# Moving columns and PSUM columns taken in other orders of 64-byte lines

## The chip, the cores and the metric

The kernel runs on one core of one Trainium2 chip. The metric is the device time of one execution in microseconds; of several executions the median is given. Nothing but the order in which TensorE takes the columns of its 256-column products differs between the two kernels.

## The reference, cut to what matters

256 tokens of width 1024 pass through two blocks, all in float32:

```python
# first block, 256 tokens and 256 of context
x  = x + 0.5 * gate * swiglu(modulate(rms_norm(x)), ffn1_w_in, ffn1_w_out)     # the context too
bg, cg, vc, q, k, v, gt = split(modulate(rms_norm(x)) @ w_in)
x  = x + gate * merge(conv_branch(bg, cg, vc), attention(q, k, v), gt)
x  = x + 0.5 * gate * swiglu(modulate(rms_norm(x)), ffn2_w_in, ffn2_w_out)
x  = rms_norm(x)
# second block
x  = x + rms_norm(concat(mlstm(...), stick_breaking(...)) @ w_out_ab)          # even layer, from x @ w_in_ab
x  = x + rms_norm((pool_mix(p) * silu(z)) @ w_out_c)                           # odd layer, from x @ w_in_c
```

Nearly all arithmetic is in the products of activations with weight matrices, each of which is used once.

## The kernel before, in words

Each float32 product is made of three products of type fp32r (float32 rounded so that TensorE takes it in one pass): weights and activations are each split into a high and a low part, and high*high, high*low and low*high are summed in PSUM. For weights, ScalarE writes the high part WH (line 1565) and VectorE the low part WL (line 1988), one "chunk" of 4 x 128 x 256 weights at a time, from a ring W of eight buffers that the SP queue fills from HBM. Activations lie turned, features on the partitions and tokens along the free axis, as pairs of buffers: XH and XL inside XHB and XLB, GH and GL (hidden layer of the two feed-forward parts), YH/YL, OH/OL, ZH/ZL, RH/RL, PH/PL.

`Plan` writes the order of all work as a list of steps. A step "ck" is one chunk of one `Gemm`. A Gemm has a kind ("fa1", "q", "cg", ...), an index i of its 256 weight columns, and `cols`, the token columns it is made for: (0, 512) in the first feed-forward part and for k and v (latent and context tokens together), 256 columns everywhere else. `chunk(s)` in the TensorE program issues it: for each 128 weight columns j and each 128 rows k three matmuls, lines 1105, 1106, 1107. The stationary operand is 128 x 128 of WH or WL (eight 64-byte lines of every partition), loaded by an LDWEIGHTS that comes with each matmul; the moving operand is one row of the activation buffer, 256 or 512 tokens of four bytes (16 or 32 lines); the output is as many columns of one PSUM bank, of four that are used in turn. A Gemm whose `turned` is false (v, ev, sv, p1) has the two roles the other way round, lines 1111 to 1113. Small products of plain float32 (attention, sums of squares, the mLSTM) stand between, on other lines.

A Gemm with eight 128-row blocks has 2 x 8 x 3 = 48 matmuls. The stages, in order of time: first feed-forward part (fa1, fb1, fx1; its last group of columns, made by `halves`, in two passes of 256 tokens) to 392 us; q, then k and v to 446; cg, vc, bg to 532; gt and mc to 593; ga to 622; ma to 644; res to 667; second feed-forward part (fa2, fb2, fx2) to 855; even layer (eq, ek, ev, eo, ez, then sq, sk, sv, sz) to 1101; p0 to 1150; odd layer (op, oz, om) to 1272; p1 to 1315.

Where the buffers start, in units of a 64-byte line (16 columns): XHB and XLB hold the first moving buffer at columns 0 and 80 and the later one, XH and XL, at columns 48 and 0. The buffers of the other stages follow a pad each in one common place: 16 columns of pad ahead of GH[1] and GL[1], 64 columns ahead of YH, of GH[2], of ZH and of RH. So GH[1] and GL[1] begin on a line of the other parity than GH[2], YH, OH, ZH, PH, XH and XL do; WH and WL stay where they are, and by the kernel's sizes lie at the same parity as GH[1] and at the other parity than the rest.

Of the kernel before, what the change touches and what calls it, by code (L numbers as in the profile page):

```python
# [15 lines left out]
T = 256  # L16
# [856 lines left out]
def build_program(nc, w, out):  # L873
    with ExitStack() as ctx:
# [95 lines left out]
        def parts(j):  # L970
# [5 lines left out]

        MOVING = {"fa1": (X1H, X1L), "fb1": (X1H, X1L), "fx1": (GH[1], GL[1]), "fx2": (GH[2], GL[2]), "mc": (YH, YL), "ma": (OH, OL), "res": (YH, YL),
                  "p0": (ZH, ZL), "p1": (RH, RL)}
        SHADE = {4: T, 5: T}
        NORMED = {1: 0, 2: 16, 3: 32, 4: 40, 5: 48}  # L980
        READY = {"fa1": ("nl", 0), "q": ("nl", 16), "fa2": ("nl", 32), "eq": ("xr", 0), "ev": ("nl", 40), "oz": ("nl", 48), "mc": ("yl", 0),
# [22 lines left out]
        def _(sp):  # L1004
# [39 lines left out]
                             X[:, 4 * j + 2 * a:4 * j + 2 * a + 2, 0:T]).then_inc(S["out"], 16)  # L1044
            sp.wait_ge(S["out"], 16 * 4)

        @block.tensor
        def _(pe):
            def ones(name, i):
# [18 lines left out]
            def chunk(s):  # L1068
                gm = s.gemm
                kind, (a, b) = gm.kind, gm.cols  # L1070
                if kind == "om":
                    xh, xl = PH[:, gm.g % 2, :, :], PL[:, gm.g % 2, :, :]
                else:
                    xh, xl = MOVING.get(kind, (XH, XL))
                _, h, l = parts(s.chunk)
                pe.wait_ge(S["wl"], s.chunk + 1)
                order = [(j, k) for j in range(len(gm.tiles)) for k in range(s.nk)]
                if gm.first:
                    order.sort(key=lambda o: o[1])
                if s.b:  # L1080
                    order = [o for o in order if o[1] == s.b - 1]
                if s.half >= 0:
                    order = order[len(order) // 2 * s.half:len(order) // 2 * (s.half + 1)]
                for j, k in order:
                    t, kk = gm.tiles[j], s.k0 + k
                    ps = P[:, t % 4, :]
                    if kk == 0 and t >= 4:
                        name, v = plan.tile_free[t - 4]
                        pe.wait_ge(S[name], v)
                    if gm.first and j == 0 and not (kind == "oz" and gm.raw):  # L1090
                        if kind in ("fa1", "fb1"):
                            pe.wait_ge(S["nl"], 2 * kk + 2)
                        elif kind == "k":
                            pe.wait_ge(S["nl"], NORMED[2] + 8 + kk + 1)
                        elif kind in ("fx1", "fx2"):
                            pe.wait_ge(S["hl" + kind[2]], gm.g + kk + 1)
                        elif kind == "om":
                            pe.wait_ge(S["pl"], 4 * gm.g + kk + 1)
                        else:
                            name, v = ("xr", 8) if kind == "op" and gm.raw else READY[kind]  # L1100
                            pe.wait_ge(S[name], v + kk + 1)
                    if gm.turned:
                        o = ps[:, 0:b - a]
                        c = slice(j * 128, j * 128 + 128)
                        pe.matmul(o, h[:, k, c], xh[:, kk, a:b], start=kk == 0, stop=False)  # L1105
                        pe.matmul(o, h[:, k, c], xl[:, kk, a:b], start=False, stop=False)  # L1106
                        mm = pe.matmul(o, l[:, k, c], xh[:, kk, a:b], start=False, stop=kk == gm.nk - 1)  # L1107
                    else:
                        o = ps[:, 0:256]
                        c = slice(a + j * 128, a + j * 128 + 128)  # L1110
                        pe.matmul(o, xh[:, kk, c], h[:, k, :], start=kk == 0, stop=False)  # L1111
                        pe.matmul(o, xh[:, kk, c], l[:, k, :], start=False, stop=False)  # L1112
                        mm = pe.matmul(o, xl[:, kk, c], h[:, k, :], start=False, stop=kk == gm.nk - 1)  # L1113
                    if kk == gm.nk - 1 or (k == s.nk - 1 and j == len(gm.tiles) - 1):
                        mm.then_inc(S["g"], 1)
                    if kk == gm.nk - 1 and kind in SUMS and (kind[:2] != "fx" or gm.g == 12):
                        m = gm.i + j if kind[:2] == "fx" else 2 * gm.i + j
                        if m == 6 or m == 7 and kind != "fx2":
                            ones(SUMS[kind], m - 6)
# [13 lines left out]
            for s in seq:  # L1133
# [5 lines left out]
                elif s.kind == "s1":  # L1139
                    pe.wait_ge(SI[1], 16)  # L1140
                    pe.wait_ge(S["sf"], 3 * s.a + 3)
                    for t in range(2):
                        for i in range(2):
                            c = T * i + 128 * t
                            mm = pe.matmul(P[:, s.a, t:t + 1], SQ1[:, s.a, 0, c:c + 128], con("one", 0, 1),
                                           start=i == 0, stop=i == 1)
# [6 lines left out]
                elif s.kind == "mm":  # L1153
                    pe.wait_ge(S["sc"], 1)
                    for r in range(2):
# [7 lines left out]
                        for k in range(4):  # L1163
                            mm = pe.matmul(ps[32 * k:32 * k + 32, 0:256], SCP[:, 4 * r + k, :], src[:, k, :],
                                           start=r == 0, stop=r == 1)
                        mm.then_inc(S["mm"], 1)
                elif s.kind == "mt":
                    pe.wait_ge(S["mr"], 2 * s.a + 2)
                    for g in range(2):
                        for j in range(2):  # L1170
                            n = 2 * g + j
                            mm = pe.transpose(ps[:, 128 * n:128 * n + 128],
                                              ROW[:, (2 * s.a + 1 - g) % 4, 128 * j:128 * j + 128], con("id"))
# [93 lines left out]
                elif s.kind == "m0":  # L1267
                    h = s.a
# [1116 lines left out]
```

## Time and profile before

| | us |
|---|---|
| median of 3 runs | 1329.38 |
| lowest, highest | 1324.02, 1330.24 |
| the profiled execution | 1324.45 |
| its span, first to last instruction | 1322.6 |
| TensorE busy | 1304.7 (99%) |
| weight loads busy | 1210.0 (91%) |
| VectorE busy, ScalarE busy | 903.0 (68%), 644.3 (49%) |

TensorE's matmuls are pipelined: each is shown longer than the distance at which they start. For 256 columns the profile shows 276 to 283 ns of duration, while the starts lie 113 to 120 ns apart. The distance from start to start, called the pitch below, is what a matmul costs in a stream.

### The profile page before, as it was taken

What the parts mean: (1) busy time and instruction counts of PE and PEld (TensorE: products, weight loads), DVE (VectorE), ACT (ScalarE), POOL (GpSimd) and SP (SyncE); (2) the same over time, 40 slices, a digit from 0 to 9 for tenths busy, and PEclk for the clock granted to TensorE, in tenths of its full rate; (3) what the DMA queues carried; (4) which work ended last, traced back from release to release, by engine and by line L of the source; (5) the groups of instructions that cost most, each with busy time, mean ns of one, the idle gap of its engine ahead of it and who ended that gap; (6) DMA issues with size and microseconds to landing.
All of it is one profiled execution on the core that took longest, in us unless ns stands there. A gap on an engine that the chain in (4) does not pass through costs nothing. (4 is left out here: it accounts for less than half of the span.)

```text
span 1322.6 us, 23508 instructions
## 1 busy us (share of the span) xinstructions
PE 1304.7 (99%) x9348; PEld 1210.0 (91%) x9348; DVE 903.0 (68%) x1455; ACT 644.3 (49%) x1027; POOL 27.3 (2%) x27
## 2 busy tenths in 40 slices
PE   9999999999999999999999999999999999999998
PEld 6788888888889999999999999989999999999998
DVE  4768775555658587554775555788887665689873
ACT  4622311222236345554555445666665765556552
POOL 0000000000010000000000000200000000100000
PEclk9999999999999999999999999999999999999999
DMA  9755555646635354545556665556546455436760
GB/s 358 270 186 191 191 191 192 222 159 215 204 107 161 111 159 130 159 128 160 178 155 194 190 201 174 171 159 184 148 143 181 128 174 176 145 112 208 217 197 33
DMA packets 201485, 230.20 MB, mean 174 GB/s; under 512 B 7073, under 2 KB 191649, under 8 KB 201377
## 3 DMA queue, kind: packets, MB, share of 16 engines
q1 hardware_dynamic: 201088, 228.42, 54.7%
q8 instruction: 75, 1.23, 0.4%
q10 hardware_dynamic: 288, 0.28, 0.1%
q14 instruction: 34, 0.27, 0.1%
HBM read 227.63 MB, written 1.05 MB: 173 GB/s over the span
## 5 line engine op out<-in xcount | busy, mean ns | idle before, releaser
L1105 PE MATMUL P<-XHB,WH 128*128 128x256 f32 (+1 forms) x1808 | 553.1, 306 | 7.4 <-DVE XLB L1784 3.9
L1106 PE MATMUL P<-XLB,WH 128*128 128x256 f32 (+1 forms) x1808 | 543.2, 300 | 0.0
L1107 PE MATMUL P<-XHB,WL 128*128 128x256 f32 (+1 forms) x1808 | 543.2, 300 | 0.0
L1988 DVE TENSOR_TENSOR WL<-W,WH 128x1024 fp32r<-128x1024 f32 x358 | 431.7, 1224 | 87.2 <-ACT WH L1565 87.0
L1565 ACT ACTIVATE WH<-W 128x1024 fp32r<-128x1024 f32 x358 | 369.0, 1042 | 249.3 <-PE P L1107 157.8
L1105 PEld LDWEIGHTS P<-XHB,WH 128*128 128x128 f32 x1808 | 340.0, 188 | 27.7 <-issue 8.2
L1106 PEld LDWEIGHTS P<-XLB,WH 128*128 128x128 f32 x1808 | 340.1, 188 | 15.2 <-issue 0.5
L1107 PEld LDWEIGHTS P<-XHB,WL 128*128 128x128 f32 x1808 | 340.2, 188 | 14.6
L1105 PE MATMUL P<-GH,WH 128*128 128x256 f32 (+1 forms) x372 | 121.2, 326 | 0.0
L1106 PE MATMUL P<-GL,WH 128*128 128x256 f32 (+1 forms) x372 | 120.6, 324 | 0.0
L1107 PE MATMUL P<-GH,WL 128*128 128x256 f32 (+1 forms) x372 | 120.6, 324 | 0.0
L1858 DVE TENSOR_TENSOR TS<-TS,P 128x512 f32<-128x512 f32 (+1 forms) x44 | 24.4, 554 | 84.1 <-PE P L1107 84.1
L1106 PEld LDWEIGHTS P<-GL,WH 128*128 128x128 f32 x372 | 70.0, 188 | 6.4 <-issue 0.2
L1105 PEld LDWEIGHTS P<-GH,WH 128*128 128x128 f32 x372 | 70.0, 188 | 6.3 <-DVE WL L1988 0.2
L1107 PEld LDWEIGHTS P<-GH,WL 128*128 128x128 f32 x372 | 70.0, 188 | 6.1
L2058 DVE CUSTOM_DVE_ANT_0 W<-W,AC,V 128x1024 f32<-128x1024 f32 x56 | 71.5, 1277 | 0.0
L1424 ACT ACTIVATE GH<-TS 128x512 fp32r<-128x512 f32 (+1 forms) x44 | 23.0, 524 | 90.1 <-DVE TS L1858 90.1
L1418 ACT ACTIVATE TS<-P 128x512 f32<-128x512 f32 (+1 forms) x44 | 21.5, 491 | 84.6 <-PE P L1107 84.5
L1868 DVE SCALAR_TENSOR_TENSOR X<-P,GM,X 128x256 f32<-128x256 f32 x48 | 21.2, 479 | 52.1 <-PE P L1107 52.0
L1111 PE MATMUL P<-WH,XHB 128*128 128x256 f32 x160 | 45.7, 285 | 1.4 <-DVE WL L1988 1.1
L1112 PE MATMUL P<-WL,XHB 128*128 128x256 f32 x160 | 44.6, 279 | 0.0
L1113 PE MATMUL P<-WH,XLB 128*128 128x256 f32 x160 | 44.6, 279 | 0.0
(322 smaller groups left out, 1797.3 us busy)
## 6 DMA issues: line engine op xcount, KB each, us to landing
W<-in_ffn_w_in SPq DMA_DIRECT2D x88, 512.0 KB, 4.8
W<-in_w_in_ab SPq DMA_DIRECT2D x72, 512.0 KB, 4.6
W<-in_w_modt SPq DMA_DIRECT2D x56, 512.0 KB, 3.9
W<-in_w_in SPq DMA_DIRECT2D x52, 512.0 KB, 4.1
W<-in_ffn_w_out SPq DMA_DIRECT2D x40, 512.0 KB, 4.8
W<-in_w_in_c SPq DMA_DIRECT2D x32, 512.0 KB, 4.3
W<-in_w_out_ab SPq DMA_DIRECT2D x16, 512.0 KB, 4.4
W<-in_w_out_c SPq DMA_DIRECT2D x16, 512.0 KB, 4.7
```

Of the source, the lines that this page charges most:

```text
L1105: pe.matmul(o, h[:, k, c], xh[:, kk, a:b], start=kk == 0, stop=False)
L1106: pe.matmul(o, h[:, k, c], xl[:, kk, a:b], start=False, stop=False)
L1107: mm = pe.matmul(o, l[:, k, c], xh[:, kk, a:b], start=False, stop=kk == gm.nk - 1)
L1111: pe.matmul(o, xh[:, kk, c], h[:, k, :], start=kk == 0, stop=False)
L1112: pe.matmul(o, xh[:, kk, c], l[:, k, :], start=False, stop=False)
L1113: mm = pe.matmul(o, xl[:, kk, c], h[:, k, :], start=False, stop=kk == gm.nk - 1)
L1418: act.activation(TS[:, f % NS, 0:n], ps, ACT.Silu).then_inc(S["sil" + kind[2]], 1)
L1424: act.activation(GH[m][:, f % 12, :], TS[:, f % NS, 0:n], ACT.Copy).then_inc(S[f"hh{m}"], 1)
L1565: act.activation(h, a, ACT.Copy).then_inc(S["wh"], 1)
L1858: dve.tensor_tensor(TS[:, f % NS, 0:n], TS[:, f % NS, 0:n], ps, ALU.mult).then_inc(S[f"hm{m}"], 1)
L1988: dve.tensor_tensor(l, a, h.bitcast(F32), ALU.subtract).then_inc(S["wl"], 1)
L2058: td = dve.tensor_tensor_reduce(a if v == s.c - 1 else JK[:, :, :], a, (AC0, AC1)[v][:, :, :], 1.0, vec("bmod", 8 * g + k), ALU.mult, ALU. ...
```

## The change

Every product in lines 1105 to 1107 that has 256 moving columns takes these columns in another order, by kind. The same order is used for the moving operand and for the PSUM output, so each column lands where it did. Products of 512 columns and those that are not turned stay. No instruction, wait or transfer is added or taken away.

```diff
+        WAYS = {"q": "even", "cg": "back", "vc": "back", "bg": "back", "gt": "pairs", "mc": "even", "ga": "quads", "ma": "pairs",
+                "res": "back", "eq": "even", "ek": "even", "ez": "back", "sq": "pairs", "sk": "pairs", "sz": "even",
+                "p0": "back", "op": "even", "oz": "pairs"}
...
+        def way(gm):
+            if gm.kind in ("fa2", "fb2"):
+                return ("plain", "even", "back", "pairs", "quads", "twos", "eights")[gm.i // 2 % 7]
+            if gm.kind == "fx2":
+                return ("even", "back", "pairs", "quads")[gm.i // 2]
+            return WAYS.get(gm.kind, "plain")
+        def in_order(a, kind):
+            if kind == "even":
+                return a.rearrange("p (l e c) -> p e l c", e=2, c=16)
+            if kind == "pairs":
+                return a.rearrange("p (l e c) -> p e l c", e=2, c=32)
+            if kind == "twos":
+                return a.rearrange("p (l e c) -> p e l c", e=2, c=2)
+            if kind == "eights":
+                return a.rearrange("p (l e c) -> p e l c", e=2, c=8)
+            if kind == "quads":
+                return a.rearrange("p (l e c) -> p e l c", e=4, c=16)
+            if kind == "back":
+                return a[:, ::-1]
+            return a
...
                         o = ps[:, 0:b - a]
+                        mh, ml = xh[:, kk, a:b], xl[:, kk, a:b]
+                        if b - a == T:
+                            o, mh, ml = (in_order(v, way(gm)) for v in (o, mh, ml))
                         c = slice(j * 128, j * 128 + 128)
-                        pe.matmul(o, h[:, k, c], xh[:, kk, a:b], start=kk == 0, stop=False)
-                        pe.matmul(o, h[:, k, c], xl[:, kk, a:b], start=False, stop=False)
-                        mm = pe.matmul(o, l[:, k, c], xh[:, kk, a:b], start=False, stop=kk == gm.nk - 1)
+                        pe.matmul(o, h[:, k, c], mh, start=kk == 0, stop=False)
+                        pe.matmul(o, h[:, k, c], ml, start=False, stop=False)
+                        mm = pe.matmul(o, l[:, k, c], mh, start=False, stop=kk == gm.nk - 1)
```

With the 16 lines of a row numbered from 0: "even" takes lines 0, 2, ... 14, then 1, 3, ... 15; "pairs" 0, 1, 4, 5, 8, 9, 12, 13, then 2, 3, 6, 7, ...; "quads" 0, 4, 8, 12, then 1, 5, 9, 13, and so on; "eights" the first half of every line, then the second halves; "twos" columns 0, 1, 4, 5, 8, 9, ..., then 2, 3, 6, 7, ...; "back" columns 255 down to 0.

## Rows read from the trace of the kernel before

**Rows 1.** The page: span, busy shares, TensorE's row and granted clock in 40 slices.
```profile
span 1322.6 us, 23508 instructions
...
PE 1304.7 (99%) x9348; PEld 1210.0 (91%) x9348; DVE 903.0 (68%) x1455; ACT 644.3 (49%) x1027; POOL 27.3 (2%) x27
...
PEclk9999999999999999999999999999999999999999
```

**Rows 2.** Waits of TensorE, the longest: total us, times, longest us.
```profile
PE P L1105 <- DVE XLB L1784: 3.9, 3, 1.5
```

**Rows 3.** TensorE in order of time, near 700 us (start us, us): second feed-forward part.
```profile
700.09 0.28 PE L1105 MATMUL P<-XHB,WH 128*128 128x256 f32 x1
...
701.45 0.28 PE L1105 MATMUL P<-XHB,WH 128*128 128x256 f32 x1
```

**Rows 4.** The same near 626 us: the products "ma".
```profile
625.75 0.28 PE L1105 MATMUL P<-OH,WH 128*128 128x256 f32 x1
...
627.52 0.28 PE L1105 MATMUL P<-OH,WH 128*128 128x256 f32 x1
```

**Rows 5.** The same near 381 us: "fx1" in passes of 256 columns.
```profile
380.73 0.28 PE L1107 MATMUL P<-GH,WL 128*128 128x256 f32 x1
...
382.53 0.28 PE L1107 MATMUL P<-GH,WL 128*128 128x256 f32 x1
```

**Rows 6.** Weight loads in 700:720, 624:640 and 378:390: busy us, mean ns.
```profile
L1107 PEld LDWEIGHTS P<-XHB,WL 128*128 128x128 f32 x60 | 11.3, 188 | 0.0
...
L1107 PEld LDWEIGHTS P<-OH,WL 128*128 128x128 f32 x45 | 8.6, 192 | 0.0
L1105 PEld LDWEIGHTS P<-OH,WH 128*128 128x128 f32 x46 | 8.6, 188 | 0.0
...
L1105 PEld LDWEIGHTS P<-GH,WH 128*128 128x128 f32 x31 | 5.9, 192 | 0.0
```

**Rows 7.** Line 1106 in nine stages, from q to the odd layer: busy us, mean ns.
```profile
L1106 PE MATMUL P<-XLB,WH 128*128 128x256 f32 x64 | 17.9, 280 | 0.0
...
L1106 PE MATMUL P<-XLB,WH 128*128 128x256 f32 x191 | 53.1, 278 | 0.0
...
L1106 PE MATMUL P<-XLB,WH 128*128 128x256 f32 x66 | 18.2, 276 | 0.0
...
L1106 PE MATMUL P<-XLB,WH 128*128 128x256 f32 x64 | 17.8, 278 | 0.0
...
L1106 PE MATMUL P<-OL,WH 128*128 128x256 f32 x64 | 18.0, 281 | 0.0
...
L1106 PE MATMUL P<-XLB,WH 128*128 128x256 f32 x336 | 92.7, 276 | 0.0
...
L1106 PE MATMUL P<-XLB,WH 128*128 128x256 f32 x429 | 119.7, 279 | 0.0
...
L1106 PE MATMUL P<-ZL,WH 128*128 128x256 f32 x127 | 35.3, 278 | 0.0
...
L1106 PE MATMUL P<-XLB,WH 128*128 128x256 f32 x224 | 61.9, 276 | 0.0
```

**Rows 8.** TensorE in order of time, products of 512 columns near 250 and 426 us.
```profile
250.06 0.39 PE L1105 MATMUL P<-XHB,WH 128*128 128x512 f32 x1
...
252.32 0.39 PE L1106 MATMUL P<-XLB,WH 128*128 128x512 f32 x1
...
425.22 0.39 PE L1107 MATMUL P<-XHB,WL 128*128 128x512 f32 x1
...
427.32 0.39 PE L1107 MATMUL P<-XHB,WL 128*128 128x512 f32 x1
```

**Rows 9.** The same, plain float32 products of 256 columns, back to back.
```profile
615.90 1.89 PE L1244 MATMUL P<-PT,VV 128*128 128x256 f32 x8
```

**Rows 10.** One line's instructions: loads of 8 weight columns, then of 128 (ns min/median/max).
```profile
L1254 PEld LDWEIGHTS P<-XHB,WH x8: 87/88/88, 861.9 to 864.3; 128*8 128x8 f32 x8
...
L1105 PEld LDWEIGHTS P<-OH,WH x64: 187/188/188, 621.7 to 644.0; 128*128 128x128 f32 x64
```

**Rows 11.** TensorE in order of time near 26 us: 16 small products with their loads.
```profile
26.10 1.07 PE L1164 MATMUL P<-WXA,SCP 128*32 128x256 f32 x16
```

## The prediction

> **What bounds the kernel now.** I read the page first. TensorE is busy for 1304.7 of 1322.6 us at the full granted clock, VectorE for 68% and ScalarE for 49% [rows 1]; the waits view shows how little TensorE waits for others, 3.9 us at the longest entry [rows 2]. So the end is set by TensorE's stream, and what a matmul costs there is its pitch, start to start. The timeline gives it. In the second feed-forward part twelve pitches take 701.45 - 700.09 = 1.36 us, 113.3 ns each [rows 3]. In "ma" fifteen take 1.77 us, 118.0 ns [rows 4]. In fx1's passes of 256 columns fifteen take 1.80 us, 120.0 ns [rows 5]. So one and the same form of matmul runs at three levels, and the durations tell them apart: 276, 281 and 283 ns.
>
> What differs is seen in the weight loads of the same stretches [rows 6]: all take 188 ns at the first level, one in three takes 192 at the second, and all take 192 at the third. I read this as the load of the next weights and the moving read meeting in SBUF and one of them being held up. The third level is found where the moving buffer begins on a line of the same parity as the weights, GH[1]; everywhere else the parity is the other one, and the level is the first or the second. So the sequence of line parities matters, and that is what the change alters.
>
> **The change part by part.** It adds no instruction. Counting the Gemms by `way`, 48 matmuls each (fx2 has 132 per column group, p0 96, and op and oz eight Gemms each), 5424 of the 6120 turned matmuls of 256 columns change: back 1668 (cg, vc, bg 576, p0 384, fa2/fb2/fx2 324, res and ez 192 each), even 1668 (eq, ek, sz 576, op 384, fa2/fb2/fx2 324, q and mc 192 each), pairs 1476 (sq, sk 384, oz 384, fa2/fb2/fx2 324, gt and ma 192 each), quads 420 (ga 192, fa2/fb2/fx2 228), twos 96, eights 96.
>
> What they cost now follows from the mean duration of line 1106 in each stage [rows 7], 276 standing for 113.3 ns, 281 for 118.0: q 116.8 (17.9/64 = 279.7), the convolution's three 115.2, gt and mc 113.3, ga 115.2, ma and res 118.0, second feed-forward part 113.3, even layer 116.1, p0 115.2, odd layer 113.3. Weighted by the counts: back 115.3, even 114.7, pairs 114.6, quads 114.2, twos and eights 113.3.
>
> No row of before has an order other than rising columns, so each order is bounded. The lower end for all: the load of 128 weight columns, (188 - 88)/120 = 0.83 ns a column [rows 10], 107 ns. The upper end: reads or writes that no longer keep the column rate, 216 ns [rows 9]. Within these I take:
> - back: it begins each row on line 15, an odd one, where all other orders begin on an even one. That gives the relation of GH[1] to the weights, level three: 120.0. (120.0 - 115.3) x 1668 = +7.8 us.
> - even and quads: the parity stays for eight or four lines while the eight weight lines go on alternating, so half of them meet and half don't; I take the middle of levels one and three, 116.7. (116.7 - 114.7) x 1668 = +3.3 us, (116.7 - 114.2) x 420 = +1.1 us.
> - pairs: the parities alternate as before, from an even line. Nothing changes: 0, between -1.9 us (all at 113.3) and +8.0 (all at 120.0).
> - twos and eights: every line is visited twice. One column time a visit makes 16 more, 6.7 ns: x 192 = +1.3 us. Upper end, at the half rate of rows 9: +19.7 us.
> - The instructions' patterns are longer. Issue isn't near its limit: 16 loads and matmuls start within 1.07 - 0.38 = 0.69 us, 46 ns a pair [rows 11]. At 0; it would show only from 113 ns a pair on.
> - The engines that read PSUM read it in rising order as before, and the weights' splitters have room (68% and 49%). What TensorE loses is not hidden by anything, since it waits for nobody; what it gains would come off the end almost whole.
>
> Sum: 7.8 + 3.3 + 1.1 + 1.3 = 13.5 us, on the profiled execution's 1324.45: 1338. That execution is 4.9 us under the median of 1329.38 and near the fastest, 1324.02; the spread may itself be the share of level two. A median after should lie between 1338 and 1343: I say 1340.
>
> [...] The loads' durations differ with the buffer and the stretch [rows 6]. The Trainium skill ("TensorE: Matmul & The Clock Gate", Step-by-step: what each phase is for) says that the weight load and the moving operand have independent read ports, so that loading the next weights steals nothing from the running matmul; by that the order couldn't matter, the sum would be 0 and the time 1324 to 1329. The three levels speak against it. [...]
>
> **The rivals.**
> 1. An order breaks the column rate. If the read or the write side fetches ahead only for rising or unbroken columns, a changed product falls toward plain float32's 216 ns. For back alone: (216 - 115.3) x 1668 = +168 us, 1492. If taking the same parity again and again is what can't be kept up, even and quads: 101 x 2088 = +211 us, 1535. If any broken PSUM pattern does it: 101 x 5424 = +548 us, 1872; I give this last case 0.03 of the rival's chance. For: 17/16 shows that the moving side is the limit already, without slack. Against: nothing in the trace shows a line order other than the plain one, and line-sized pieces are large.
> 2. Faster: the new orders undo the meetings. With all changed products at 113.3 the gain is 2.0 x 1668 + 1.4 x 1668 + 0.9 x 420 + 1.3 x 1476 = 7.9 us, 1316.5. If also the column time a line comes from two neighbouring lines in turn and goes with another order, up to 6.3 x 5424 = 34 us more, 1282, where the weight load becomes the bound. It decides once the changed products average under 113.6 ns, 1.2 less than now. For: more than a third of the products are above the first level. Against: 113.3 never gives way to less in the trace, and the load and the stream already fit there without a loss.
> 3. Nothing: which level holds is a matter of phase after an interruption, not of parity, and the column time a line stays. Then 1324 to 1330. For: levels one and two occur with the same buffers and parities. Against: GH[1].
>
> **How the numbers follow.** The forecast, and what is near it up to all changed products at 120 ns (28.3 us, 1353 on the profiled time, 1358 on the median), 0.43. Rival 3, 0.24. Rival 2, 0.17. Rival 1, 0.16. About 0.5%, 6.6 us, is what a measurement can tell from no change. Faster by more: 0.16 of rival 2 and 0.03 of rival 3, 0.19. Within: 0.20 of rival 3, 0.01 of rival 2 and 0.04 of the forecast's low side, 0.25. Slower: 0.39 + 0.01 + 0.16 = 0.56. The forecast's own range is 1333 to 1358. The range to hold 8 in 10 reaches down to rival 2's first case as a median, 1316.5 + some of the 4.9 = 1318, and up to all at 120 with twos and eights at half rate, 1353 + 19.7 = 1372; what is left out is rival 1's larger cases and the column time a line gone.
>
> **What would show it.** In the profile after, the timeline gives a pitch for each order, best in fa2 and fb2, where neighbouring groups of columns differ in it and all stood at 113.3: back there at 120 with all loads at 192 ns, even and quads between, pairs at 113.3, twos and eights at 120. Products of 512 columns and p1 must stay. The forecast is wrong in its mechanism if back stays at 113.3, or if even differs from pairs by nothing; it is wrong in size if any order goes past 121.

## The result, and the profile after

The changed kernel takes 1361.58 us (median of four executions; 1361.47 to 1361.93), the kernel before, run beside it, 1326.7 us (four executions, 1323.04 to 1330.24): a ratio of 1.0264, with a 95% interval of 1.0229 to 1.0298. The change makes the kernel 2.6% slower. The profiled execution took 1361.47 us, 37.0 more than the one before (1324.45).

The page after; these rows answer to [rows 1]:
```profile
span 1359.7 us, 23508 instructions
...
PE 1343.4 (99%) x9348; PEld 1246.8 (92%) x9348; DVE 904.4 (67%) x1455; ACT 644.5 (47%) x1027; POOL 27.1 (2%) x27
...
PEclk9999999999999999999999999999999999999999
```
The instructions are the same in number, the clock is full, VectorE and ScalarE are busy as long as before. TensorE is busy for 38.7 us more, and the span grew by 37.1. The longest wait is the one of [rows 2]:
```profile
PE P L1135 <- DVE XLB L1814: 3.9, 3, 1.5
```
So nothing waits more; the matmuls themselves stand farther apart. (Pitch levels are named as in the prediction: level one is 113.3 ns, level two 117.8 to 118.0, level three 120.0.) In fa2 and fb2, all at 113.3 ns before [rows 3], neighbouring groups of columns differ in their order. The kernel after in eight stretches, by window: even, back, pairs, quads, twos, eights, plain (the group after eights), and p1, which isn't turned. Columns: the window, its us and TensorE's busy us (matmuls seen in it), clock, DMA share, GB/s:
```profile
693.00:703.00 10.00, 10.00 (x85) 1.00 0.81 254
704.00:714.00 10.00, 10.00 (x87) 1.00 0.60 185
716.00:726.00 10.00, 10.00 (x85) 1.00 0.65 205
727.00:737.00 10.00, 10.00 (x86) 1.00 0.61 182
739.00:759.00 20.00, 20.00 (x89) 1.00 0.33 106
795.00:805.00 10.00, 10.00 (x86) 1.00 0.60 185
807.00:817.00 10.00, 10.00 (x88) 1.00 0.64 201
1310.00:1350.00 40.00, 40.00 (x342) 1.00 0.22 68
```
Since matmuls overlap, a window also shows the two or three already under way. For even, 10 us / (85 - 2.3) = 121 ns; for twos 20 us / (89 - 1.8) = 229 ns, with the DMA share at 0.33 where its neighbours have about 0.6: weights are used up half as fast. For p1, 40 us / (342 - 2.4) = 117.8 ns, though its instructions are the old ones.

Single starts give the pitch exactly. TensorE after in order of time, near 745 us (twos):
```profile
744.75 0.41 PE L1136 MATMUL P<-XLB,WH 128*128 128x256 f32 x1
...
746.36 0.41 PE L1137 MATMUL P<-XHB,WL 128*128 128x256 f32 x1
```
Seven pitches in 1.61 us, 230 ns. And near 720 us (pairs):
```profile
720.26 0.28 PE L1137 MATMUL P<-XHB,WL 128*128 128x256 f32 x1
...
721.10 0.28 PE L1135 MATMUL P<-XHB,WH 128*128 128x256 f32 x1
```
Seven in 0.84 us, 120.0 ns.

The weight loads of the same stretches answer to [rows 6]: line 1136 (1106 of before) in even, back, pairs, twos, eights and plain; busy us, mean ns:
```profile
L1136 PEld LDWEIGHTS P<-XLB,WH 128*128 128x128 f32 x28 | 5.3, 189 | 0.0
...
L1136 PEld LDWEIGHTS P<-XLB,WH 128*128 128x128 f32 x29 | 5.4, 188 | 0.0
...
L1136 PEld LDWEIGHTS P<-XLB,WH 128*128 128x128 f32 x28 | 5.3, 188 | 0.0
...
L1136 PEld LDWEIGHTS P<-XLB,WH 128*128 128x128 f32 x28 | 5.8, 208 | 0.6
...
L1136 PEld LDWEIGHTS P<-XLB,WH 128*128 128x128 f32 x29 | 5.5, 191 | 0.0
...
L1136 PEld LDWEIGHTS P<-XLB,WH 128*128 128x128 f32 x29 | 5.6, 192 | 0.0
```
In these windows even and pairs are slower than the plain stretch beside them and back is as slow, but their loads aren't held up: 188 and 189 ns on all three lines, as at level one before. Plain at level two has 192 on one line of three (here 1136) and 188 on the other two, so back, at the same 117.8 ns, doesn't look like it in the loads. What costs there is not what I had read from the loads.

Over both traces, the mean distance of starts by order (stretches without interruption):

| products | count | before, ns | after, ns | us | forecast, us |
|---|---|---|---|---|---|
| even | 1668 | 114.9 | 121.4 | +10.8 | +3.3 |
| twos | 96 | 113.3 | 229.2 | +11.1 | +0.6 |
| pairs | 1476 | 114.8 | 120.0 | +7.6 | 0 |
| back | 1668 | 115.1 | 117.9 | +4.7 | +7.8 |
| quads | 420 | 114.0 | 119.9 | +2.4 | +1.1 |
| eights | 96 | 113.3 | 120.0 | +0.6 | +0.6 |
| 256 columns, unchanged | 1560 | 115.2 | 117.4 | +3.4 | 0 |
| 512 columns, unchanged | 1572 | 227.0 | 227.0 | 0 | 0 |

The sum is 40.6 us; the span grew by 37.1, so some 3.5 us came back in gaps between. (The last column sums to 13.4; the prediction rounds to 13.5.)

### The profile page after: what moved, and what is told of

The parts are those of the page before. It is cut to its first block, busy times and chain, and to the rows that moved or that the text cites. A ratio compares the mean times of both kernels' runs of the same rounds, so it can differ in the third digit from the quotient of the medians.

```text
span 1359.7 us, 23508 instructions
## 1 busy us (share of the span) xinstructions
PE 1343.4 (99%) x9348; PEld 1246.8 (92%) x9348; DVE 904.4 (67%) x1455; ACT 644.5 (47%) x1027; POOL 27.1 (2%) x27
## 4 chain that ended last, share of the span: by engine, by line
PE 90%; DVE 6%; ACT 2%; issue 1%; DMA 1%; DVEq 0%; SPq 0%; ACTq 0%
PE P L1135 25%; PE P L1136 25%; PE P L1137 25%; PE P L1141 2%; PE P L1143 2%; PE P L1142 2%; DVE WL L2018 1%; PE P L1274 1%; PE P L1262 1%; DVE TS L1940 1%; DMA X<-in_ctxt 1%; PE P L1092 1%; PE P L1194 1%; DVE TS L1802 1%; PE P L1267 1%
## 5 line engine op out<-in xcount | busy, mean ns | idle before, releaser
L1135 PE MATMUL P<-XHB,WH 128*128 128x256 f32 (+1 forms) x1808 | 563.6, 312 | 6.1 <-DVE XLB L1814 3.9
L1137 PE MATMUL P<-XHB,WL 128*128 128x256 f32 (+1 forms) x1808 | 554.6, 307 | 0.0
L1136 PE MATMUL P<-XLB,WH 128*128 128x256 f32 (+1 forms) x1808 | 554.5, 307 | 0.0
L1137 PE MATMUL P<-GH,WL 128*128 128x256 f32 (+1 forms) x372 | 121.7, 327 | 0.0
```

The costliest lines, as they stand in the source:

```text
L1135: pe.matmul(o, h[:, k, c], mh, start=kk == 0, stop=False)
L1136: pe.matmul(o, h[:, k, c], ml, start=False, stop=False)
L1137: mm = pe.matmul(o, l[:, k, c], mh, start=False, stop=kk == gm.nk - 1)
```

## The experiments

The code common to them lets the read side (r) and the PSUM side (v) have orders of their own, and adds orders: "fours" (blocks of four lines, the 1st and 3rd, then the 2nd and 4th), "octs" (lines 0, 8, then 1, 9, ...), "lback" (lines backward, columns in a line forward), "cback" (lines forward, columns in a line backward), "bits" (every second 16-byte run of four columns, then the rest), "swap" (the two halves), "lswap" (neighbouring lines exchanged).

### Reads or writes

```diff
+            n = ORDERS[gm.i // 2 % 11]
+            return {"fa2": (n, "plain"), "fb2": ("plain", n)}.get(gm.kind, ("plain", "plain"))
...
+                        r, v = way(gm)
+                        o = in_order(ps[:, 0:b - a], v)
+                        mh, ml = in_order(xh[:, kk, a:b], r), in_order(xl[:, kk, a:b], r)
```

> The kernel before, but in the second feed-forward part each pair of column groups has one order: fa2 takes it for the moving read alone (PSUM in plain order), fb2 for the PSUM write alone (moving read plain); groups 2 to 20 in turn even, back, pairs, quads, twos, eights, lines backward (each line forward), columns backward within each line, twos of four columns (16 bytes), fours (four lines at a time). The token columns of these products land permuted. Theory A (SBUF read): fa2 shows the changed kernel's pitches, even 121.3, back 117.8, pairs and quads 120.0, eights 120.0, twos 229 ns, and fb2 stays at 113.3 or 117.8. Theory B (PSUM write): the reverse, fa2 at 113.3 or 117.8 and fb2 at those. Theory C: each side costs a share, most of all in twos, and neither alone reaches the sum.

One execution took 1334.22 us (before: 1328.12). Windows, each pair first with the order read, then with it written: even, back, pairs, twos; last, bits read:
```profile
687.00:692.00 5.00, 5.00 (x44) 1.00 0.72 219
693.00:697.00 4.00, 4.00 (x38) 1.00 0.75 241
698.00:703.00 5.00, 5.00 (x45) 1.00 0.44 123
704.00:708.00 4.00, 4.00 (x38) 1.00 0.84 275
709.00:714.00 5.00, 5.00 (x44) 1.00 0.40 116
715.00:719.00 4.00, 4.00 (x37) 1.00 0.88 278
732.00:741.00 9.00, 9.00 (x41) 1.00 0.46 147
743.00:747.00 4.00, 4.00 (x38) 1.00 0.32 91
...
815.00:820.00 5.00, 5.00 (x45) 1.00 0.36 108
```
From single starts, read: even 121.3 ns, back 117.8, pairs and quads 120.0, twos 229.3, eights 120, lback 117.9, cback 133.2, bits 117.8, fours 113.3. Written: 113.3 to 113.9, but 117.8 for pairs and lback, a level that plain products have too. In the rows, twos read is 9 us / (41 - 1.8) = 230 ns; twos written 4 us / (38 - 2.4) = 112, within one count of 113.3. The costs are on the read side; nothing that the written orders show is more than a plain level.

### The writes alone, in the whole kernel

```diff
-                            o, mh, ml = (in_order(v, way(gm)) for v in (o, mh, ml))
+                            o = in_order(o, way(gm))
```

> The changed kernel with its orders on the PSUM write alone, moving reads plain; the token columns land permuted. Theory A (only the read costs): as the kernel before, 1322 to 1331 us, every order at 113.3 or 117.8 ns, twos too. If a PSUM pattern that isn't contiguous cost anything at these rates: 20 us or more over before.

Over 5424 products PSUM is written in other orders: 1324.7 us against 1324.41, ratio 1.0013 (1.0002 to 1.0023). Its ten executions fall into two groups, seven near 1324.6 and three near 1329.8 us. The kernel before showed such groups in other sessions (1323.04 to 1330.24 above), but all 29 of its executions in this one lay between 1323.61 and 1324.9; so these runs don't exclude that orders in PSUM make the upper group likelier. The profiled one took 1329.76 and had the second feed-forward part at 117.8 ns. Twos, written only, in it:
```profile
L1136 PE MATMUL P<-XLB,WH 128*128 128x256 f32 x27 | 7.6, 281 | 0.0
```
281 ns is level two, as in "ma" before [rows 7], not a level of this order. So PSUM's order has no price of its own here beyond 0.2%: at the half rate, twos alone would have cost 11 us. And one stage at level two instead of one, 1584 matmuls x 4.5 ns = 7 us, is of the size of the 5.3 us between the two groups of times; which stages stood at level two in the executions that have no profile isn't known.

### The parity

Every moving buffer of 256 columns starts on the parity of the weights.
```diff
-        X1H, XH = (XHB[:, a:a + 4096].rearrange("p (k t) -> p k t", k=8) for a in (0, 48))
-        X1L, XL = (XLB[:, a:a + 4096].rearrange("p (k t) -> p k t", k=8) for a in (80, 0))
+        X1H, XH = (XHB[:, a:a + 4096].rearrange("p (k t) -> p k t", k=8) for a in (0, 32))
+        X1L, XL = (XLB[:, a:a + 4096].rearrange("p (k t) -> p k t", k=8) for a in (80, 16))
...
-            sbuf(st, "PAD3", [128, 64])
+            sbuf(st, "PAD3", [128, 48])
```
(PAD5, PAD6 and PAD7 the same.)

> The kernel before with all 256-column moving buffers begun one line further or nearer, so that they have the parity of the weights, and in fa2 and fb2 the changed kernel's seven orders; all else plain. Theory M: plain goes to 120.0 ns everywhere (about 25 us more in all), back, which now begins on the other parity, gets to 113.3 or 117.8 or stays at 117.8, even and pairs stay within 2 ns of 121.3 and 120.0. Theory J: the orders keep their pitches of the changed kernel and only plain moves.

One execution: 1360.58 us. Windows: even, back, pairs, and p1 (plain):
```profile
693.00:702.00 9.00, 9.00 (x77) 1.00 0.75 237
704.00:713.00 9.00, 9.00 (x79) 1.00 0.57 181
715.00:725.00 10.00, 10.00 (x85) 1.00 0.58 181
...
1310.00:1350.00 40.00, 40.00 (x340) 1.00 0.21 67
```
Plain went to 118.7 in p1 and 120.0 in the second feed-forward part: for plain order the parity counts, as the prediction had read from GH[1]. In p1 the moving side is WH and WL, which stayed in place, and only the stationary RH and RL moved; so it is the position of one side against the other that counts. Back, pairs, quads and twos stayed, at 117.8, 120.0, 120.0 and 228.9; even came to 120.0 (for 121.4), eights to 117.0 (for 120.0). At this parity even, pairs and quads cost nothing over plain, and back and eights are 2 to 3 ns faster than plain: what an order costs over plain isn't a constant of the order. Back begins on the parity of the weights in the changed kernel and on the other one here, and stands at 117.8 in both; level three, which the prediction gave it, it never has. This run alone can't tell a price of back from level two, which is what the other parity allows; its loads, above, speak for a price.

The products "k", 512 columns from XH and XL, went the other way: 228.8 ns on average here against 233.5 before, and fa1, fb1 and fx1, which lie at the parity of the weights in both kernels, take 226.7. For 512 columns in plain order the parity of the weights is the faster one, which a meeting of lines of one parity doesn't explain.

### How the cost grows: 512 columns

```diff
+            n = ORDERS[gm.i // 2 % 11] if gm.kind in ("fa1", "fb1") else "plain"
+            return n, n
```

> The kernel before with orders on the 512-column products fa1 and fb1 (32 moving lines, the same 8 weight lines): groups 2 to 20 even, back, pairs, quads, twos, eights, lines backward, columns backward in each line, fours, eighths. Plain is 226.7 ns there. Theory M: an order costs at most what it costs on 256 columns, since the load is as long: even +8, pairs and quads +6.7, back +4.5. Theory J: twice that, +16, +13.3, +9, since there are twice the lines. Twos about 458 and eights 240 under both.

One execution: 1356.04 us. Windows: even, back, pairs, twos, cback:
```profile
54.00:75.00 21.00, 21.00 (x89) 1.00 0.73 255
77.00:97.00 20.00, 20.00 (x87) 1.00 0.63 210
99.00:120.00 21.00, 21.00 (x90) 1.00 0.59 200
...
145.00:186.00 41.00, 41.00 (x92) 1.00 0.30 102
...
299.00:322.00 23.00, 23.00 (x88) 1.00 0.54 183
```

| over plain, ns | even | pairs | quads | back | eights | octs | cback | fours | twos |
|---|---|---|---|---|---|---|---|---|---|
| 256 columns (113.3) | 8.1 | 6.7 | 6.7 | 4.5 | 6.7 | 6.7 | 20 | 0 | 116 |
| 512 columns (226.7) | 13.3 | 10 | 12.8 | 6.7 | 6.7 | 4.6 | 40 | 0 | 227 |

The weights are the same eight lines in both. Cback and twos double exactly: a cost of the moving read, 1.25 ns for each line read backward in it. Even, pairs, quads and back grow by 1.5 to 1.9 times; eights and octs don't grow. One limit: fa1 and fb1 read buffers at the parity of the weights, the 256-column products of the first row buffers at the other one, so the rows differ in parity too, and for the small costs the growth isn't shown to come from the length alone. 233.3 ns, the pitch of back and eights, is also the plain level of "k".

### Small weight loads

fa2 loads 8 weight columns in place of 128 (two lines of it; 120 of its 128 output rows are left out). In the second kernel groups differ in the load too.
```diff
+                        if kind == "fa2" and gm.i:
+                            c, o = slice(j * 128, j * 128 + 8), in_order(P[0:8, t % 4, 0:b - a], v)
```

> The kernel before, but fa2's groups 2 to 20 load only 8 of 128 weight columns (so 120 rows of their output are left out), in the orders even, back, pairs, quads, twos, eights, lines backward, columns backward in each line, plain, eighths (lines 0, 8, 1, 9, ...); fb2 has full weights in other orders: lines backward, columns backward in each line, 16-byte twos, plain, fours, halves swapped, neighbouring lines swapped, eighths, quads, plain. Theory M (the weight load's read meets the moving read): with hardly any load all whole-line orders fall to 113.3 ns, eights and twos stay above. Theory J (the jump itself costs the moving read): the light products keep 120.0 for pairs and quads, 121.3 for even, 117.8 for back. In fb2 M gives 113.3 to 121.3 depending on how the parities of neighbouring lines alternate: eighths like even (121), fours under pairs (114 to 117), neighbouring lines swapped 120.

One execution: 1336.03 us. With loads of 8: even 121.7, back and lback 117.9, pairs 118.4, quads 113.9, twos 233, eights 116.2, cback 133.2, octs 119.9, plain 116.75. With full loads, in fb2: lswap and octs 120, quads 119.7, lback 117.8, bits 117.7, cback 133.2, fours and swap 113.4. Neither theory has plain at 116.75 beside quads at 113.9, so a second kernel took plain and quads at several loads.

> The kernel before, but fa2 and fb2 load fewer weight columns (the rows of output above them are left out) in one order a group: 2 plain with 8, 4 plain with 32, 6 plain with 64, 8 quads with 8, 10 quads with 32, 12 quads with 64, 14 pairs with 8, 16 even with 8, 18 back with 8, 20 plain with 8. Theory M for quads (their cost is meeting the load, whose reads last as long as there are columns): 113.3 with 8, rising with the columns to 120 with 128; theory J for even and back (their cost is in the moving read itself): 121 and 117.8 with 8 as with 128. Pairs between. Plain 113.3 with any load, or 117.8 in a phase.

One execution: 1327.84 us. Windows: plain with 8, quads with 8, quads with 64, pairs, even, back with 8, and plain with 8 again, a last time:
```profile
687.00:696.00 9.00, 9.00 (x82) 1.00 0.81 251
...
720.00:729.00 9.00, 9.00 (x79) 1.00 0.67 200
...
775.00:784.00 9.00, 9.00 (x79) 1.00 0.62 192
786.00:795.00 9.00, 9.00 (x78) 1.00 0.62 188
797.00:806.00 9.00, 9.00 (x77) 1.00 0.56 179
809.00:818.00 9.00, 9.00 (x79) 1.00 0.57 176
820.00:829.00 9.00, 9.00 (x80) 1.00 0.62 192
```
By single starts 113.3, 117.8, 116.7, 118.3, 120.0, 117.8 and 116.7; quads with 32 columns took 117.8, plain with 32 and 64 took 113.3. Even, back, octs, cback and twos keep nearly their whole cost with hardly a load to meet, and pairs most of it; of the 6.7 ns of eights 2.9 are left. The forecast for quads, 113.3 with 8 and rising with the load, failed: 117.8, 117.8, 116.7 and 119.7 to 120.0 for 8, 32, 64 and 128 columns don't rise steadily. Two things don't fit either theory: quads with 8 came at 113.9 in one kernel and at 117.8 in the other, plain with 8 at 113.3 and at 116.7.

### What a read fetches

fa2 and fb2 read the same columns several times, or start 8 or 4 bytes off (sums of other columns).
```diff
+            n = 2 if how[:4] == "off2" else 1 if how == "off1" else 0
+            v = x[:, kk, a - n:b - n]
+            if how == "quad4":
+                return v[:, 0:64].rearrange("p (q c) -> p q c", c=4).unsqueeze(2).broadcast_to([128, 16, 4, 4])
```

> The kernel before, but in fa2 and fb2 the moving read, not the PSUM write, takes: group 2 each run of 4 columns (16 bytes) four times, 4 the same twice, 6 each column four times, 8 one 64-byte line 16 times, 10 the first half row twice; groups 12 to 18 read from two columns (8 bytes) to the left, plain, in 16-byte runs of every second, in half lines, in even and odd lines; group 20 plain from one column to the left. The sums of these products are other than the reference's. Theory F (the read fetches 16-byte pieces, one per 113.3/64 = 1.77 ns, as often as the order enters a piece): the first three are no longer bound by fetches, 107 to 110 ns (the load's 107), line and half row stay at 113.3; shifted plain has 65 pieces, 115.1; shifted 16-byte runs 128 pieces, 227; shifted half lines 96, 170; shifted even 80, 142; one column to the left 65, 115.1. Theory L (one column time for each 64-byte line entered, and twos slow for another reason): groups 2 and 6 under 110, 4 about 110, all shifted ones under 125.

One execution: 1344.44 us. Windows: runs of four columns four times each, one line 16 times; then 8 bytes off (two columns to the left): plain, bits, half lines, even:
```profile
686.00:695.00 9.00, 9.00 (x83) 1.00 0.83 256
...
718.00:728.00 10.00, 10.00 (x86) 1.00 0.60 190
...
773.00:783.00 10.00, 10.00 (x85) 1.00 0.62 193
785.00:805.00 20.00, 20.00 (x89) 1.00 0.33 105
807.00:821.00 14.00, 14.00 (x86) 1.00 0.41 131
824.00:834.00 10.00, 10.00 (x71) 1.00 0.54 170
```
Count the aligned 16-byte pieces that a row enters. Plain has 64, at 113.3: 1.77 ns each. Bits, 8 bytes off, breaks every run in two, 128 pieces: 227 by that, 230 measured. Half lines off: 96, 170 against 166.7. Even off: 80, 142 against 145. Twos enters 128: 227 against 229. So large losses go by 16-byte pieces. The small ones don't: plain 8 bytes or one column off has 65 pieces, 115.1 by the rule, and measured 120.0; one line over and over, 64 pieces, 120.0. A row that is 4 or 8 bytes off also begins on the 64-byte line before, which has the parity of the weights, and 120.0 is what plain order takes at that parity; the run doesn't separate the two. Reading a quarter or half of the pieces, each several times, was forecast at 107 to 110 ns and came to 111.7 in all three ways.

### Twos taken back

```diff
-                return ("plain", "even", "back", "pairs", "quads", "twos", "eights")[gm.i // 2 % 7]
+                return ("plain", "even", "back", "pairs", "quads", "plain", "eights")[gm.i // 2 % 7]
```

> The changed kernel with the one order twos (96 matmuls in fa2 and fb2, group 10) put back to plain. Ledger from pitches: 96 x (229.3 - 113.3 to 117.8) = 10.7 to 11.1 us less, 1350.5 to 1351. If twos only filled time that others would take, less than 5 us.

1349.77 us (1349.62 to 1350.35), ratio to before 1.0166 (1.0128 to 1.0204): 11.8 us under the changed kernel, where 10.7 to 11.1 was expected. 96 of 9348 matmuls carried about a third of the loss.

### Can an order end level two?

Plain 256-column products stand at 113.3 or 117.8 for whole stages. In the trace of before they change at an interruption (other products or a wait between), or where the two sides change roles (ev to eo or ez, sv to sz), and not within a stream. Here the first three matmuls of some Gemms take another order (FIRST names it by kind and group).
```diff
+            n = FIRST[gm.kind][gm.i % 4] if gm.kind in FIRST and j == 0 and kk == 0 else "plain"
+            return n, n
```

> The kernel before, with another order only in the first three matmuls of a group of columns (j = 0, k = 0), all else plain: ma even, quads, twos, eights; res halves swapped, fours, 16-byte runs, back; sq even, sk fours, sz quads, eq twos, cg eighths. If the second level (117.8) is only a phase between load and read, one of these puts the rest of the group at 113.3 where the kernel before stands at 117.8 (ma, res, most of sq, sk, sz), 4.5 ns x 45 = 0.2 us a group. If the level belongs to the buffers or the time, all stay at 117.8 and ma and res take as long as before.

One execution: 1333.54 us. TensorE in "ma", after a triple of quads, order of time; it stood at 118.0 there before [rows 4]:
```profile
634.82 0.28 PE L1133 MATMUL P<-OH,WH 128*128 128x256 f32 x1
...
635.73 0.28 PE L1135 MATMUL P<-OH,WL 128*128 128x256 f32 x1
```
Eight pitches in 0.91 us, 113.8. The next group of "ma" begins with a triple of twos, with no interruption between:
```profile
639.01 0.28 PE L1133 MATMUL P<-OH,WH 128*128 128x256 f32 x1
...
640.07 0.28 PE L1133 MATMUL P<-OH,WH 128*128 128x256 f32 x1
```
Nine pitches in 1.06 us, 117.8: the triple put the stream back to level two. By single starts, the groups of "ma" went from 117.8 to 117.8 (even), from 117.8 to 113.3 (quads), from 113.3 to 117.8 (twos) and from 117.8 to 113.3 (eights); all four stood at 117.8 before. Elsewhere twos ended level two once in a stream (eq, group 2) and started it once (eq, group 3), octs started it once (cg, group 3), and fours, where level two stood, left it (three groups of sk). Quads in three groups of sz, behind an interruption, gave 113.4 where before had 117.8. "res" then ran wholly at 113.3, left so by "ma", but fa2, gt and mc came out at 117.8. So for plain order the two levels are a phase: it is kept until something disturbs it, and three matmuls in another order can be that something, in either direction.

Four kernels in the plain order then tried this for gain. The first two have quads in the first three matmuls, or in the first alone, after each interruption (69 places), on the moving and on the PSUM side. The edit of the one with the first alone:
```diff
+                        n = ("quads",) * 1 if fresh[0] and b - a == T else ()
+                        n += ("plain",) * (3 - len(n))
+                        fresh[0] = 0
...
+                if s.kind in OTHERS:
+                    fresh[0] = 1
```

> The kernel before, all in plain order but for the first three matmuls after any other product (69 places), turned or not, which take the order quads on both sides. In the run before this the quads put the stream to 113.3 ns from either level, at 30 to 45 ns each time. Theory P (the second level is a phase that the last interruption leaves, and quads end it): the share of 256-column matmuls above 116 ns falls from a third (some 2300 x 4.45 = 10 us) to under a tenth; less 69 x 0.04 = 3 us spent: 5 to 8 us faster, ratio 0.994 to 0.996. If quads only happened to fall well there: within 2 us of before, share of the second level a third as before.

> The same with the order quads in the first matmul alone. If one changed read is enough to move the load against the read: as the run with three, and 1 to 2 us better for the smaller price. If the phase needs several: the second level stays where it was, time within 2 us of before.

Three matmuls: 1325.01 us, ratio 1.0021 (1.0007 to 1.0034), where 5 to 8 us less were expected; ma, res and sz fell to 113.3 to 113.9, but gt, p0, ga and oz rose, and 36% of the 256-column matmuls stood above 116 ns, against 34% before. One: 1325.35, ratio 1.0006 (0.9991 to 1.0021); most stages at 113.3, but in the profiled execution the whole second feed-forward part at 117.8, which makes 38%. That stage came out at 117.8 in the write-only kernel too, whose reads are all plain, so it isn't shown to be the odd read's doing. The next two add places where no interruption is: first fa2 and fb2 alone, then the start of every group of q, v, the even layer and p0 as well (103 places in all).
```diff
-                        n = ("quads",) * 1 if fresh[0] and b - a == T else ()
+                        n = ("quads",) * 1 if (fresh[0] or again(gm, j, kk)) and b - a == T else ()
```

> The kernel of the single quads read, with one more such read at the start of two column groups of the second feed-forward part, fb2 group 0 and fa2 group 2, behind the waits of its first group. There that kernel's profile stood at 117.8 ns for all 1584 matmuls, 7 us. Theory P: they fall to 113.3 in every execution and the spread of 1319 to 1331 us closes to its low end: 1319 to 1320, ratio 0.995 to 0.997. If the level belongs to the execution and not to the phase: still two groups of times 7 us apart.

> The same with a single quads read also at the start of every column group of q, v, all of the even layer and p0 (some 50 more, at 10 to 15 ns, 0.6 us), where waits inside a group can leave the second level. Theory P: those stages, now at 114 to 117.8, fall by 1 to 2 ns a matmul, 2 to 3 us less than the run above; v and sv, whose moving side is the weights, show whether quads act there too. If quads from the first level can also lead to the second: no gain or a loss of up to 2 us.

The first: 1324.9 us, ratio 0.9963 (0.9936 to 0.9991), where 1319 to 1320 and an end of the spread were expected. Its twelve times still run from 1319.21 to 1331.61. In its profile the second feed-forward part stands at 113.3, but it did so already ahead of the two added reads, and op and oz came out in part, om and p1 wholly at 117.8. The second: 1322.56, ratio 0.9949 (0.9921 to 0.9976), the lowest median here, about 0.5% under before; its share above 116 ns is some 19%, v, sv and ev still stand at 117.8, and its times run from 1319.74 to 1331.78.

What one quads read does shows in the profile of the second kernel. Turned products that began with one in a stream unbroken for eleven matmuls or more, at level two, went to 113.3 in two places (sq, groups 4 and 6) and stayed in five (eq, groups 2 and 3, ek and ez, group 2, sk, group 4); those that began at level one stayed there. Where the weights are the moving side it went the other way: ev, groups 0 and 3, and sv, group 4, went from 113.3 to 117.8 at their quads read. For ev, group 0:
```profile
873.38 0.28 PE L1143 MATMUL P<-WH,XHB 128*128 128x256 f32 x1
...
874.91 0.28 PE L1144 MATMUL P<-WL,XHB 128*128 128x256 f32 x1
```
Thirteen pitches in 1.53 us, 117.7; the products ahead of it stood at 113.3, and in the trace of before this group does too. Behind an interruption level one became more frequent: "ma" and "res" stood at 113.3 to 113.6 in the profiles of all four kernels and at 117.8 in those of before and of the write-only kernel.

The gain itself depends on the session. Beside the last two kernels the one before ran from 1323.95 to 1336.75, median 1329.4; beside the first two it ran at 1324.41, and against that 1322.56 would be 0.1% less.

## Why the prediction was wrong, step by step

**Right.** TensorE's pitch sets the end, nothing hides a loss in it, and most of the loss reaches the end (40.6 us of pitches, 37.1 of span). Issue and PSUM's readers cost nothing, as taken. The sign is as forecast, and the time lies in the range; the likeliest value was 21.6 us too low. The last paragraph had named the test: "it is wrong in size if any order goes past 121". Even and twos did.

**Where the sum failed.** It gave 13.4 us for pitches that lost 40.6. The terms were too low by 10.5 us (twos), 7.6 (pairs), 7.5 (even) and 1.3 (quads), 3.4 us of unchanged products weren't in it, and back was too high by 3.1.

**"twos and eights ... One column time a visit makes 16 more, 6.7 ns".** The step that failed most: twos took 116 ns more. I had taken the 64-byte line as the unit of a read, since 17/16 fits it; for large losses the unit is the 16-byte piece. The half rate of [rows 9], 216 ns, was my upper end, and twos went past it, to 229.2. Eights took exactly 6.7 more, but by luck: one column time a visit would be 13.3 ns with 512 columns, where eights took 6.7, and at the other parity it stood at 117.0. The Trainium skill ("SBUF — State Buffer", the box on cachelines under Door 1) has the 16 bytes, and says that two hits in a row are enough. The experiment with shifted runs agrees on the 16 bytes; on the two hits, twos makes exactly two per piece and runs at 229 ns, so here they are not.

**"pairs ... Nothing changes: 0".** 120.0, +7.6 us, near my bound of 8.0. The argument was that line parities go on alternating. The parity does count for plain order (113.3 to 118.7 and 120.0 when shifted), but not for pairs, the same at either parity.

**"even and quads ... I take the middle of levels one and three".** 121.4 and 119.9 for 116.7. For even the cost isn't a meeting of half the lines with the load: it stays with 8-column loads (121.7 and 120.0). For quads the small loads gave 113.9, 117.8 and, with 64 columns, 116.7, and leave it open.

**"back ... gives the relation of GH[1] to the weights, level three".** 117.9, not 120.0, loads at 188 and not 192 ns. The step also had the wrong ground: the parity of the line on which back begins doesn't set its pitch, 117.8 at either. It was too high by 3.1 us, which hid a part of the other errors.

**What wasn't in the sum.** Unchanged 256-column products gained 3.4 us: om and p1 at level one before and at two after, p1 as 40 us / (342 - 2.4) above. Rival 3's premise holds for plain products: which of the first two levels holds is a phase. It does not hold for even, pairs, quads and back, each of which stood within 1 ns of one pitch in every stage of the changed kernel. By single starts 34% of the 256-column matmuls lay above 116 ns before, 88% after.

**A reading of before.** The prediction took 226 ns for 512 columns as undisturbed and 233 in "k" as disturbed. The undisturbed ones (fa1, fb1, fx1) are those at the parity of the weights, "k" is at the other, and the shifted buffers brought it to 228.8. So at 512 columns the parities trade places, and the meeting of loads and reads by parity, on which the terms for even, quads, pairs and back were built, doesn't cover it.

**Rivals.** Rival 1's price (216 ns) came true for one order of six, twos, and by its read. Its PSUM case (any broken pattern) is refuted: 1.0013 (1.0002 to 1.0023). The Trainium skill ("Advanced Engine Details and Errata", PSUM Cachelines) says both that any pattern that isn't contiguous slows matmuls significantly and that every two consecutive elements should be contiguous for best throughput; the write-only kernel, all of whose orders keep two neighbours together, contradicts the first and agrees with the second. Rival 2 had no order under 113.3; only repeated reads of the same pieces went to 111.7.

**Open.** Why whole-line orders differ from each other (fours 0, back 4.5, pairs and quads 6.7, even 8.1 ns), why these differences vanish against plain at the other parity, and which of them are costs of the read alone. What sets the phase, and so level one or two, in a given execution. Why one odd read ends level two at some places and not at others. Whether orders in PSUM make the upper group of times likelier. Whether a row that begins off a 16-byte boundary is slow by that or by the line it begins on. Why plain and quads with 8-column loads came at two values.

## What to carry to other kernels

Take the moving operand's columns in rising order, in runs of whole 16-byte pieces that begin on a 16-byte boundary; an order that takes each piece in two visits halves the rate, and 96 such matmuls cost 11 us here. Have the order on PSUM's side if an order is needed: 5424 products cost 0.02 to 0.23% there, against 2.6%. When durations in one stream come in two near levels, look for what ran just before the stretch; such a phase may be worth more than the edit that is tested (7 us of stage against 4.7 us for 1668 products backward). A size that comes out right for one case, as for eights, is no proof of the rule: try it at a second length before building a sum on it.

## What the runs showed of the hardware

- Reading 256 columns backward through a whole row takes 117.8 ns for 113.3; backward inside each 64-byte line with lines forward, 133.2, and 40 ns more with 512 columns.
- Large losses of the moving read go by the aligned 16-byte pieces that an order enters, about 1.8 ns each: 64 pieces 113.3 ns, 80 145, 96 166.7, 128 229 to 230.
- A moving row that starts one column (4 bytes) or 8 bytes ahead of its 64-byte line runs at 120.0 ns.
- The position of the moving rows relative to the stationary operand, by 64-byte line, is worth 5.4 to 6.7 ns a matmul of 256 columns in plain order (113.3 to 118.7 or 120.0), -1.4 for even, -3 for eights and nothing for back, pairs, quads and twos; with 512 columns the other parity is the slow one (233.5 against 226.7).
- One matmul that reads quads ended level two in two of seven places in a stream and started it in three of weights as the moving side. Three matmuls in another order can move a stream of plain 256-column products from 117.8 to 113.3 ns (quads, eights, twos) or from 113.3 to 117.8 (twos, octs). The level then stays until something disturbs it again.
